# A decoder layer on one core: input and residual in feature-major order, the norm's factor applied where PSUM is emptied

## The reference, cut to what matters

```python
def rmsnorm(x, g):
    y = xf * lax.rsqrt(jnp.mean(xf * xf, axis=-1, keepdims=True) + EPS)
    return (y * g.astype(jnp.float32)).astype(x.dtype)
...
h = rmsnorm(x, g_mix[l])
(nq, nkc, nvc, nks, nvs, nkw, nvw, ngt, mq, mk, mv, mo, mi, mf) = split_cols(h @ w_in[l], IN_SIZES)
...
x = x + mixed @ w_out[l]            # and so for the memory attention and the MLP
```

## Time and profile before

| | |
|---|---|
| median of 3 runs | 1942.45 us (1942.35 to 1943.73) |
| the profiled execution | 1937.9 us |
| its span in the trace | 1936.2 us |
| mean granted clock of PE | 0.978 of full speed |
| busy: PE, DVE, POOL, ACT | 94%, 64%, 35%, 28% of the span |

### The profile page before, as it was taken

The page is one execution under the profiler, slowest core; times in us unless marked ns, Lnnn a source line. Parts: engine busy times, 40 slices in busy tenths (PEclk is TensorE's granted clock), DMA queues, the critical chain, the costliest instruction groups (busy, mean ns, idle before and its releaser), DMA issues.

```text
span 1936.2 us, 24939 instructions
## 1 busy us (share of the span) xinstructions
PE 1816.0 (94%) x8892; PEld 1498.3 (77%) x8892; DVE 1245.0 (64%) x1610; ACT 534.5 (28%) x1012; POOL 672.1 (35%) x446
## 2 busy tenths in 40 slices
PE   4999799999999987989999898999999999999996
PEld 3887688877888876878777687888888888888884
DVE  4343568776877776364334536677777777777767
ACT  4104577775323232142112213111111111111112
POOL 2333344443343212401221342343443434444340
PEclk9998999999999999989999999999999999999998
DMA  6232010110111112114110111111111111111112
GB/s 156 68 107 44 23 34 23 34 44 1 55 54 43 43 65 87 44 55 141 33 32 22 33 45 35 51 44 54 43 50 48 43 54 43 53 45 43 54 33 87
DMA packets 150429, 100.07 MB, mean 52 GB/s; under 512 B 13450, under 2 KB 142686, under 8 KB 150370
## 3 DMA queue, kind: packets, MB, share of 16 engines
q1 hardware_dynamic: 143146, 86.70, 15.2%
q10 hardware_dynamic: 7224, 12.60, 2.0%
HBM read 90.88 MB, written 8.40 MB: 51 GB/s over the span
## 4 chain that ended last, share of the span: by engine, by line
PE 85%; DVE 7%; ACT 3%; issue 2%; DMA 2%; SPq 1%; POOL 0%; DVEq 0%; ACTq 0%
PE ps L635 23%; PE ps L638 22%; PE ps L639 22%; PE ps L785 3%; PE ps L847 2%; PE ps L756 2%; PE ps L945 2%; PE ps L804 1%; PE ps L805 1%; PE ps L924 1%; PE ps L757 1%; PE ps L674 1%; DVE h_lo L1396 1%; DVE nsa_shift L1540 1%; ACT pt_hi L1139 1%
## 5 line engine op out<-in xcount | busy, mean ns | idle before, releaser
L635 PE MATMUL ps<-h_hi,w_hi 128*128 128x512 f32 x1520 | 596.3, 392 | 14.8 <-DVE h_lo L1395 6.3
L638 PE MATMUL ps<-h_lo,w_hi 128*128 128x512 f32 x1520 | 593.6, 391 | 0.0
L639 PE MATMUL ps<-h_hi,w_lo 128*128 128x512 f32 x1520 | 593.3, 390 | 0.0
L562 POOL TENSOR_TENSOR w_hi<-w_raw,ones 128x1024 fp32r<-128x1024 f32 x117 | 229.9, 1965 | 1033.2 <-PE ps L635 1019.2
L635 PEld LDWEIGHTS ps<-h_hi,w_hi 128*128 128x128 f32 x1520 | 286.6, 189 | 78.9 <-issue 7.5
L639 PEld LDWEIGHTS ps<-h_hi,w_lo 128*128 128x128 f32 x1520 | 286.5, 188 | 60.1
L638 PEld LDWEIGHTS ps<-h_lo,w_hi 128*128 128x128 f32 x1520 | 286.4, 188 | 59.7 <-issue 0.7
L565 POOL TENSOR_TENSOR w_lo<-w_raw,w_hi 128x1024 fp32r<-128x1024 f32 x117 | 312.9, 2674 | 9.2
L1932 DVE TENSOR_TENSOR x_t<-ps,x_t 128x1024 f32<-128x1024 f32 x176 | 215.2, 1224 | 30.8 <-PE ps L639 30.8
L1922 DVE SCALAR_TENSOR_TENSOR fc<-fu,fw,fc 128x1024 f32<-128x1024 f32 x88 | 212.5, 2414 | 31.0 <-ACT fc L1318 29.4
L587 POOL TENSOR_SCALAR probs<-probs,nsa_inv,gate_sig 128x640 f32<-128x640 f32 (+7 forms) x128 | 100.7, 787 | 174.0 <-DVE nsa_inv L1552 173.8
(11 more groups left out here) (269 smaller groups left out, 2424.4 us busy)
## 6 DMA issues: line engine op xcount, KB each, us to landing
w_raw<-in_w_up SPq DMA_DIRECT2D x44, 512.0 KB, 3.8
w_raw<-in_w_in SPq DMA_DIRECT2D x26, 512.0 KB, 3.8
w_raw<-in_w_down SPq DMA_DIRECT2D x22, 512.0 KB, 3.5
q_st<-q_dram SPq DMA_DIRECT2D x64, 128.0 KB, 3.0
x_tok<-in_x SPq DMA_DIRECT2D x8, 512.0 KB, 7.5
w_raw<-in_w_out SPq DMA_DIRECT2D x8, 512.0 KB, 3.7
x_half<-in_x ACTq DMA_DIRECT2D x2, 2048.0 KB, 9.7
w_raw<-in_w_mem_k SPq DMA_DIRECT2D x8, 512.0 KB, 3.7
```

The lines of the kernel that those rows point to most:

```text
L562: pool.tensor_tensor(w_hi[s][:, :], w_raw[s][:, :], ones[:, :].to_broadcast([P, KT * P]), ALU.mult).then_inc(w_hi_made.sem, w_hi_made.up())
L635: ins = mm(out_ap, whi, x_hi, start=first, stop=False)
L638: mm(out_ap, whi, x_lo, start=False, stop=False)
L639: return mm(out_ap, wlo, x_hi, start=False, stop=last)
```

## The change

- Weights, parameters and x are rearranged before the launch: `w_tiles` holds each tile as 128 rows of 4 KB, `params` all gains, taps and position terms in one block, `x_rows` is x transposed, 8 blocks of 128 features by 1024 positions.
- Opening: ACT and DVE split x times g_mix as it lands, without the norm. PE runs the first two tiles (compressed keys and values) k by k with their four chunks open at once; their weights have buffers of their own (`wf_*`) and are split by ACT and DVE. Squares of x are added up beside that, `token_sums` follows the two tiles, and `spread_roots` stands between the halves of the third tile (the gates). POOL begins its splits when all of x is split.
- The factor per position, `r_in`, is multiplied in wherever DVE empties a chunk of a first projection: `kvp` (whose position terms are added in two operations of their own), gate rows, queries (`scaled_q`), keys (`scaled_k`), values, and in the mLSTM loop u_raw, mv_feat and o_gate. ACT's high parts of queries and keys come from the scaled copy.
- The ring before the attention has six banks; the gates are projected third, then two tiles of queries, then the compression, then the other five tiles.
- Residual: ACT's queue loads `x_t` in one DMA of 4 MB after the last mLSTM head. The transposes of x_half and the copies go.
- SP loads all tiles after the eleventh in one loop. The store of m_rows is issued before the attention.
- The later spreads use the column in two parts of fp32r (`col_r`), 16 matmuls, in place of a float32 one.

```diff
-            for i in range(TT):
-                sp.dma_start(x_tok[:, i, :], x_v[:, i, :]).then_inc(
...
+            sp.dma_start(par[:, :], params[:, :]).then_inc(t("gains_loaded", 16).sem, 16)
+            load_first(0)
+            load_x(0)
+            load_x(1)
+            load_first(1)
+            for k in range(2, KT):
+                load_x(k)
...
+            x_split.add(KT)
+            pool.wait_ge(x_split.sem, x_split.value())
             split_tile(0)
...
-            for half in range(2):
-                x_scaled.add(4)
-                pe.wait_ge(x_scaled.sem, x_scaled.value())
-                for k in range(KT):
-                    transposes([(x_tok[:, 4 * half + j, k * P:k * P + P], P, j * P) for j in range(4)])
...
+            def spread_roots():
+
+                pe.wait_ge(r_col_ready.sem, r_col_ready.next())
+                for j in range(TT):
+                    for part in range(2):
+                        last = mm(ps[:, 6 + j // 4, (j % 4) * P:(j % 4 + 1) * P],
+                                  col_r[:, part, j:j + 1].to_broadcast([P, P]), ident_r[:, :],
+                                  start=part == 0, stop=part == 1)
...
+            for k in range(KT):
+                pe.wait_ge(x_split.sem, x_split.next())
+                for z in range(FIRST):
+                    if k == 0:
+                        pe.wait_ge(wf_split.sem, wf_split.next())
+                    w = (wf_hi[z][:, k * P:k * P + P], wf_lo[z][:, k * P:k * P + P])
+                    for c in range(2):
+                        cs = slice(c * HALF, c * HALF + HALF)
+                        last = product(ps[:, 2 * z + c, :], w, h_hi[:, k, cs], h_lo[:, k, cs], k == 0, k == KT - 1)
...
+            token_sums(acc_x, 6)
+            gemm_tile(h_hi, h_lo, after_half=spread_roots)
+            for _ in range(2):
                 gemm_tile(h_hi, h_lo)
...
+            pe.wait_ge(t("kvp_ready").sem, t("kvp_ready").value())
...
-            xh_loaded.add(2)
-            pe.wait_ge(xh_loaded.sem, xh_loaded.value())
-            for k in range(KT):
-                for half in range(2):
-                    transposes([(x_half[half][:, j, k * P:k * P + P], P, j * P) for j in range(4)])
...
+            for k in range(KT):
+                x_square(k)
+                if k + 2 < KT:
+                    x_high(k + 2)
+            norm_root()
...
+            hm_taken.add(1)
+            act.wait_ge(hm_taken.sem, hm_taken.value())
+            act.dma_start(x_t[:, :, :], x_rows.rearrange("k p s -> p k s")).then_inc(xh_loaded.sem, xh_loaded.up())
...
+            first_low(0)
+            x_low(0)
+            x_low(1)
+            first_low(1)
+            for k in range(KT):
+                if k + 2 < KT:
+                    x_low(k + 2)
+                add_square(k % 2, acc_x, sq_x)
...
+                    tt(scaled_k[c][:, :], ps[:, b, :], r_in[:, cs], ALU.mult).then_inc(chunk_freed.sem, chunk_freed.up())
+                    dve.wait_ge(chunk_freed.sem, chunk_freed.value())
...
+                stt(scaled_q[n % 4][:, :], ps[:, b, :], DH ** -0.5, r_in[:, cs], ALU.mult, ALU.mult).then_inc(
...
-                    dve.tensor_copy(u_raw[:, 4:4 + SEQ], both(b)).then_inc(chunk_freed.sem, chunk_freed.up(2))
+                    tt(u_raw[:, 4:4 + SEQ], both(b), r_in[:, :], ALU.mult).then_inc(chunk_freed.sem, chunk_freed.up(2))
```

More of the change, by code:

```diff
@@ L463, in _, with load_first @@
-            for i in range(4):
-                load(win[:, C_Q + P * i:C_Q + P * i + P])
-            for c in (C_VS, C_VW, C_KS, C_KW):
-                load(win[:, c:c + P])
-            load(win[:, C_MQ:C_MQ + P])
-            load(win[:, C_MK:C_MK + P])
+                sp.dma_start(w_raw[s][:, :], w_tiles[n].rearrange("a p m -> p (a m)") if not isinstance(n, int)
+                             else w_tiles[FIRST + n, :, :]).then_inc(loaded[s].sem, loaded[s].up())
+            def load_first(z):
+                sp.dma_start(wf_raw[z][:, :], w_tiles[z, :, :]).then_inc(t(f"wf_loaded{z}", 16).sem, 16)
@@ L689, in _, with token_sums @@
-            for half in range(2):
-                x_scaled.add(4)
-                pe.wait_ge(x_scaled.sem, x_scaled.value())
-                for k in range(KT):
-                    transposes([(x_tok[:, 4 * half + j, k * P:k * P + P], P, j * P) for j in range(4)])
-            freed_now()
-            for _ in range(3 + NH // 2 + 2):
+            def token_sums(squares, bank):
+                sq_used.add(2 + KT)
+                pe.wait_ge(sq_used.sem, sq_used.value())
+                for j in range(TT):
+                    last = mm(ps[:, bank, j:j + 1], squares[:, j * P:j * P + P], ones[:, :], start=True, stop=True)
+                last.then_inc(sums_ready.sem, sums_ready.up())
@@ new lines, in add_square, with columns_start, columns_end @@
+            def add_square(u, total=acc, squares=sq):
+                dve.wait_ge(sq_ready.sem, sq_ready.next())
+                dve.wait_ge(sq_used.sem, sq_used.value())
+                tt(total[:, :], total[:, :], squares[u][:, :], ALU.add).then_inc(sq_used.sem, sq_used.up())
+            def columns_start(bank):
+                dve.wait_ge(sums_ready.sem, sums_ready.next())
+                dve.tensor_copy(col[:, :], ps[:, bank, 0:TT]).then_inc(col_ready.sem, col_ready.up())
+            def columns_end():
@@ L1413, in _ @@
[L1413 to L1419 removed]
+                dve.tensor_copy(col_r[:, 0, :], col[:, :]).then_inc(vector_chain.sem, vector_chain.up())
@@ L1488, in _ @@
                 b = chunk(2)
-                dve.tensor_copy(v_feat[:, br, :], both(b)).then_inc(chunk_freed.sem, chunk_freed.up(2))
-            for kv in range(2):
-                b = chunk()
-                dve.tensor_copy(hid[:, kv, :, :].rearrange("h g n -> h (g n)"), ps[0:CMP_HID, b, 0:G * NCMP]).then_inc(
-                    chunk_freed.sem, chunk_freed.up())
+                tt(v_feat[:, br, :], both(b), r_in[:, :], ALU.mult).then_inc(chunk_freed.sem, chunk_freed.up(2))
+            for q_stored in (t("q_stored0", 16), t("q_stored1", 16)):
+                q_stored.add(NH // 2)
+                dve.wait_ge(q_stored.sem, q_stored.value())
             low_keys(0)
```

511 lines of the change are left out of this document (248 added, 263 removed).

## The result

The changed kernel takes 1897.72 us in the median of four runs (1896.90 to 1901.35), the kernel before 1942.40 in the four beside them: a ratio of 0.9773, 95% interval 0.9756 to 0.9790. Forecast were 1900.0 us, 1889 to 1911. The profiled execution took 1897.03 us with a span of 1895.3, so the two profiles are 40.9 us of span apart, and the medians 44.7: the profile of before came from a quick execution.

What follows compares the result with a forecast made beforehand. TensorE, busy 94% of the span, was taken as the bound, so only its work or few waits counted. -28.3 + 3.6 + 0.7 - 0.9 - 16.9 + 0.4 - 1.0 = -42.4 gave 1900.0 us, range 1889 to 1911.

Steps and rivals of the forecast that it cites:

- The opening: Kernel start: products begin near 9.0 us without x's scaling and transposes, two tiles end at 33.0, not 61.3; -28.3 us.
- the forecast by the shared port: Opening's last three adds of squares: they wait out GpSimd's two passes, ending near 33.9; sum 0.9 us worse, 1900.9.
- the one by rows: Opening's last three adds of squares: at 2.27 us each they end at 32.3, under PE's 33.0; cost 0.
- Sums and spread: Opening on PE: new token sums and spread of the reciprocal root, 1.8 us each; +3.6 us (3.4 to 5.4).
- The scaling at the exit from PSUM: VectorE emptying first projections' PSUM, kvp included: 0 on the path, bound +15 if kvp takes three times as long.
- the first rival: Opening bound by VectorE after the root: kvp slowed by two strided inputs and GpSimd; 1904 to 1915 us, chance 0.11.
- Key multiply and bank wait: Before attention: exposed multiply of the last key half, +0.7 us; six-bank ring ends a bank wait between transposes, -0.9 us.
- The residual: Output tiles after the mixer: 64 transposes and eight copies go, next tile starts at 748.6, not 765.45; -16.9 us.
- The DMA issue ahead of the root: After the last head: ScalarE's x_t load issue stands between the last sum of squares and the root; +0.4 us.
- Weights: Key and value stage: 4 KB rows shorten five waited-for landings by 0.2 us each; -1.0 us (-2.5 to 0).
- The sum: Whole kernel: all terms total -42.4 us, from median 1942.45 to 1900.0, or profiled 1937.9 to 1895.5.
- The predicted signs: New profile: first product near 9 us, gapless, 430 ns at first; compression near 69; first output tile ending near 724.

Runs made afterwards that it cites:

- the warm TensorE: Kernel after with an early ScalarE table load and 18 products of a tile of zeros on TensorE before its first real product: 1897.01 us, ratio 0.9772.
- the doubled multiply: Kernel after with each of the sixteen kvp multiplies done twice, first into an unused tile: 1908.38 us, ratio 0.9824.
- the experiment: Kernel after with the residual as before (x loaded again in two halves, transposed on TensorE and copied): 1911.43 us, ratio 0.9843.
- The expectation above: Written for the kernel after with the four z tiles of the feed-forward part 32 bytes higher in SBUF: 1904.66 us, ratio 0.9805.
- the kernel after's second run: The kernel after measured once more with nothing changed, to show the size of chance: 1895.33 us, ratio 0.9757.
- the early table load: Kernel after with ScalarE first copying one column of zeros, so its table loads ahead of the first weights: 1897.93 us, ratio 0.9778.
- six edits: Kernel after plus early table load, warm TensorE, second first-weights before x1, GpSimd's gate split later, root before x_t issue, identity products after last head: 1895.80 us.

## Why the prediction was right, point by point

**The opening, -28.3: measured -27.2.** The road is the one described, and one step was missing: ScalarE's table load of 1.28 us stood at nothing in the sum. It alone put the first product at 10.24; weights and x0 landed as reckoned (5.18 and 6.44, against 5.2 and 6.5), and with the load out of the way PE began at 9.06 and 9.08. The low clock lasted about as long as taken (4.8 us against 4.4), which is partly luck, as other profiles of this opening have 2.7 to 6.1. The token sums waited for nothing, although the three adds took 7.39 us; they ended at 32.9, where the forecast by the shared port had them at 33.9 and the one by rows at 32.3. The Trainium skill's rule (SBUF — State Buffer, "Who interferes with whom") agrees in kind: with GpSimd out of the way the adds took 3.87. It needs PE to be earlier to cost anything, as the warm TensorE showed.

**Sums and spread, +3.6: measured 3.7** (1.84 and 1.90). The root lay under the gate tile's first half as said, though with little to spare: a cast of eight columns took 1.63 us.

**The scaling at the exit from PSUM, 0: measured 0.2, with hardly any margin left.** A kvp piece takes 1.03, not the 0.69 of the form before, and takes it also while GpSimd is idle (54 to 60 us). So it is not GpSimd; that the second strided input makes it dearer is likely but was not tried apart. That is half of the first rival. The start was misread too: the forecast had it at 41, where its own terms give 33.0 + 1.8 + 5.44 + 1.8 + 1.2 = 43.2, and it stood at 44.77. The two together ate the margins: for the compression 1.3 us were left of the 7, and for the first bank nothing of the 1.2, PE being held some 0.2 us at 49.01. That this term came out at nearly 0 is luck: had pieces and start cost 1.3 us more in all, the rival would have begun to cost in full, as the doubled multiply showed.

```profile
L1498 DVE TENSOR_TENSOR kvp<-ps,r_in 64x512 f32<-64x512 f32 x12 | 12.3, 1028 | 0.2
```

**Key multiply and bank wait, +0.7 and -0.9: measured +1.1 and -0.6** (the lead is 23.2 where the values are turned, 23.8 at the next tile and 22.8 at the first maximum).

**The residual, -16.9: measured -16.8** between the two profiles at the second output tile, if the 1.0 us more from the root to the end of the first output tile is counted apart, and 15.6 to 17.0 by the experiment. The x_t load was hidden with 28 us to spare.

**The DMA issue ahead of the root, +0.4: measured +1.7.** This step failed in size. The issue was costed as its own 0.41; that the table load would lose its cover with it was not seen, though the timeline of before had the load hidden in this very place.

**Weights, -1.0: measured -1.8** in the key and value stage, within its bounds (-2.5 to 0).

**Not in the sum: -3.8 in the feed-forward part.** Tiles that are now kept for the whole kernel (ident_r and col_r, 576 bytes, less 224 by a smaller parameter tile and a smaller col) moved every later tile up by 352 bytes, and the down products went from 233 to 229 ns. The expectation above speaks of the parameter tiles alone, which is not the whole of it. Three kernels that moved z back to slow places gave 2.9 to 4.0 us of that stretch back. By itself this would have put the forecast at 1896.

Against it stand small losses: 1.3 us between the memory attention and the feed-forward sums, and 0.9 up to the first down product, where the token sums ran at the lower clock (3.57 us in place of 2.68). The first was also there in the kernel after's second run, but not with the early table load nor with six edits: from PE's first query product to those sums it is 256.0 us before, 257.3 and 257.4 in the two runs of the kernel after, 256.2 in those two variants and up to 259.0 in others. So it goes at least in part by the execution.

**The sum, -42.4: measured -40.9 between the profiles, -44.7 between the medians.** That it came so near is partly luck. Against the 3.8 us that nobody foresaw, and 0.8 more than taken from the weights, stand 1.1 us in the opening, 1.0 in the sums, keys and bank wait together, 1.3 at the root, 1.0 by the clock in the first output tile, and the 1.3 and 0.9 just named; smaller shifts give 0.5 back. And the forecast carried over the 4.5 us by which the profile of before lay under its median; the kernel after's lay only 0.7 under its own. So the profile came 1.5 us over its forecast (1897.03 against 1895.5) and the median 2.3 under (1897.72 against 1900.0).

The predicted signs: first product near 9 (10.2), gapless (yes), 430 ns at first (yes), compression near 69 without a wait (70.9, none), first output tile ended near 724 (728: 2.1 us less lead from the opening with its sums, keys and bank wait, 1.3 from the root, 1.0 from the clock in this tile), second one right behind (yes).

## What to carry to other kernels

Count the table loads, and ask of every instruction put between a wait and an ACTIVATE which table the ACTIVATE needs: here the load then stood behind the wait, and a DMA issue of 0.4 us cost 1.7. When two things end at nearly the same time (adds and products), taking one away wins only the gap to the next: 1.8 us of some 3. A single profile can mislead: a landing that was 0.8 us late in one execution made the table load look like a third of the late start, and two more kernels with the same edit showed it to be nearly all of it. And holding an engine back to speed up another can put a short wait before TensorE: 0.66 us became 2.2 with the lower clock behind it, in the one profile that has it.

## What the runs showed of the hardware

- The place of a moving operand changes TensorE's pace by 2%: 229 ns per product of 512 columns with z at 64 over a multiple of 128 bytes, 233 at 96 and at 0. The h tiles run at 227 at a multiple of 128, where z has its 233, so the distance from a multiple of 128 alone can't be the rule. What it is stays open; it was tried at three places only.
- A cast of 128x8 with both sides in SBUF took 1.63 us while GpSimd's pass of 1.89 ran, from 36.85 until its end, and 0.17 when GpSimd was idle (33.52 in the kernel with six edits). The Trainium skill (SBUF — State Buffer, "Who interferes with whom") says that casts, copies and tensor_scalar can take the port pair that GpSimd uses, and that the later one blocks until the other ends. The trace agrees, also in the mem_tok scaling: 1885 and 2883 ns beside GpSimd, 745 and 754 alone in the kernel before.
- The granted clock in the windows reads 1.00 for the first 20 us, where products 0.43 us apart show the lower level.
- The time goes with the mean granted clock: the kernel with six edits had spans of 1889.4 us at 0.978 and 1897.4 at 0.974. Effects under some 3 us were to be read only in the timelines, not in the medians.
